# Four edits in a two-block transformer kernel: an own place for the first pair of expert rows, stream banks for memory's values, DVE for the table of rates, heads' steps ahead of channels' steps

## The reference, cut to what matters

```
# first block: mixer, then the expert layer
h   = rmsnorm(x, g_mix);   m = rmsnorm(mem, g_mem)
q, k, v, xl, gl, qm, gate = split(h @ w_in);   km, vm = split(m @ w_mem_kv)
y0 = windowed attention(rope(q), rope(k), v, sink)          # 6 heads
xc = depthwise_conv(xl)                                     # 4 taps
log_a = -8 * sigmoid(xc @ w_r + b_r) * softplus(-lam)       # lam: 2 x 768 learned numbers
y1 = gelu(gl) * (scan forward + scan backward of a = exp(log_a), sqrt(1-a^2) * i * xc)
y2 = softmax(qm @ km.T / sqrt(128)) @ vm                    # 4 heads, 256 memory rows
x  = x + (sum of sigmoid(gate_n + b) * (y_n @ p_n)) @ w_out
h2 = rmsnorm(x, g_ffn)                                      # PEER: 8 heads, top 16 of 128 x 128 experts
x  = x + sum over the picked experts e of gate_e * gelu(h2 . u_e) * v_e
# second block, twice: hybrid_layer
x  = rmsnorm(x, g_final)
z  = rmsnorm(x, norm1) @ w_in
ya = retention(4 heads);  yb = 31-tap conv, layer norm, silu;  yc = gelu, layer norm, 256 x 256 mixing;  yd = windowed attention, 8 heads
x  = x + (sum of sigmoid(gate_n) * (y_n @ w_branch_n)) @ w_out
x  = x + (silu(h @ w_gt) * (h @ w_up)) @ w_ffn_out
```

## Time and profile before

| | |
|---|---|
| median of three runs | 2144.68 us (2143.9 to 2147.41) |
| the profiled execution's own time | 2145.49 us |
| its span | 2144.2 us |
| PE busy | 2113.1 us (99%) |
| DVE, ACT, POOL busy | 65%, 58%, 46% |
| mean granted PE clock | 0.998 |

### The profile page before, as it was taken

One profiled execution on the slowest core, in us unless ns is written; L12 is line 12 of the kernel. 1 busy time (PEld: TensorE's weight loads), 2 busy tenths in 40 slices (PEclk: granted clock), 3 DMA queues, 4 the chain that ended last, 5 costly groups with the idle time before them and its releaser, 6 DMA issues.

```text
span 2144.2 us, 37243 instructions
## 1 busy us (share of the span) xinstructions
PE 2113.1 (99%) x14292; PEld 1958.1 (91%) x14292; DVE 1395.7 (65%) x2706; ACT 1247.4 (58%) x2272; POOL 977.1 (46%) x791
## 2 busy tenths in 40 slices
PE   7999999999999999999999999999999999999999
PEld 7999989999999998888889899998888999998887
DVE  4467655998676756666667765557764864757874
ACT  5669454546777865455445465746555465756553
POOL 4776557999667650000004785660001876661000
PEclk9999999999999999999999999999999999999999
DMA  6444565655444456666665554555565645455565
GB/s 231 149 138 129 172 197 173 196 178 180 145 140 147 141 168 204 195 192 192 195 195 196 186 157 139 155 180 167 187 205 158 189 146 168 141 165 177 187 194 160
DMA packets 103952, 370.59 MB, mean 173 GB/s; under 512 B 11480, under 2 KB 12896, under 8 KB 103264
## 3 DMA queue, kind: packets, MB, share of 16 engines
q1 hardware_dynamic: 103776, 368.21, 54.8%
HBM read 366.05 MB, written 2.11 MB: 172 GB/s over the span
## 4 chain that ended last, share of the span: by engine, by line
PE 88%; DVE 6%; ACT 2%; POOL 1%; issue 1%; DMA 1%; SPq 0%; DVEq 0%; ACTq 0%; POOLq 0%
PE stream_bank L568 14%; PE stream_bank L570 14%; PE stream_bank L569 14%; PE side_bank L568 9%; PE side_bank L570 9%; PE side_bank L569 9%; PE side_bank L577 4%; PE stream_bank L577 4%; PE side_bank L574 2%; PE stream_bank L574 2%; PE side_bank L918 1%; PE side_bank L917 1%; POOL unit_lo L2606 1%; ACT unit_hi L1181 1%; PE side_bank L746 1%
## 5 line engine op out<-in xcount | busy, mean ns | idle before, releaser
L2606 POOL TENSOR_TENSOR unit_lo<-raw,unit_hi 128x512 fp32r<-128x512 f32 (+1 forms) x724 | 938.5, 1324 | 943.6 <-ACT unit_hi L1181 941.6
L1181 ACT ACTIVATE unit_hi<-raw 128x1024 fp32r<-128x1024 f32 (+1 forms) x678 | 708.9, 1046 | 199.5 <-PE side_bank L570 66.0
L1777 DVE TENSOR_TENSOR unit_lo<-raw,unit_hi 128x1024 fp32r<-128x1024 f32 (+1 forms) x316 | 390.3, 1236 | 227.9 <-ACT unit_hi L1181 225.9
L568 PE MATMUL stream_bank<-hT,unit_hi 128*128 128x256 f32 x1360 | 398.9, 293 | 1.8 <-POOL unit_lo L2606 1.8
L570 PE MATMUL stream_bank<-hT,unit_lo 128*128 128x256 f32 x1360 | 384.6, 283 | 0.0
L569 PE MATMUL stream_bank<-hT,unit_hi 128*128 128x256 f32 x1360 | 384.5, 283 | 0.0
L568 PE MATMUL stream_bank<-h2T,unit_hi 128*128 128x256 f32 x1024 | 293.3, 286 | 0.0
L570 PE MATMUL stream_bank<-h2T,unit_lo 128*128 128x256 f32 x1024 | 289.8, 283 | 0.0
L569 PE MATMUL stream_bank<-h2T,unit_hi 128*128 128x256 f32 x1024 | 289.6, 283 | 0.0
L568 PEld LDWEIGHTS stream_bank<-hT,unit_hi 128*128 128x128 f32 x1360 | 259.9, 191 | 3.6 <-POOL unit_lo L2606 2.0
L569 PEld LDWEIGHTS stream_bank<-hT,unit_hi 128*128 128x128 f32 x1360 | 260.0, 191 | 1.6
(11 more groups left out here) (392 smaller groups left out, 4303.9 us busy)
## 6 DMA issues: line engine op xcount, KB each, us to landing
raw<-in_peer_u_dram SPq DMA_DIRECT2D x128, 512.0 KB, 3.5
raw<-in_peer_v_dram SPq DMA_DIRECT2D x128, 512.0 KB, 4.1
raw<-in_gate_dram SPq DMA_DIRECT2D x64, 512.0 KB, 3.5
raw<-in_gt_dram SPq DMA_DIRECT2D x44, 512.0 KB, 3.5
raw<-in_up_dram SPq DMA_DIRECT2D x44, 512.0 KB, 3.5
raw<-in_ffn_out_dram SPq DMA_DIRECT2D x44, 512.0 KB, 3.5
raw<-in_branch_dram SPq DMA_DIRECT2D x32, 512.0 KB, 3.5
raw<-in_w_gate_dram SPq DMA_DIRECT2D x24, 512.0 KB, 3.5
```

The lines of the kernel that those rows point to most:

```text
L568: mm(out, l.hi, r.hi, start=start, stop=False)
L1181: activation(k.unit_hi[n % SPLIT_SLOTS][:, 0:w], k.raw[n % RAW_SLOTS][:, 0:w], ACT.Copy).then_inc(k.sem("unit_hi"), 1)
L1777: V.tensor_tensor(k.unit_lo[s][:, 0:w], k.raw[n % RAW_SLOTS][:, 0:w], k.unit_hi[s][:, 0:w], ALU.subtract).then_inc(unit_lo, 1)
L2606: last = G.tensor_tensor(k.unit_lo[s][:, cols], k.raw[n % RAW_SLOTS][:, cols], k.unit_hi[s][:, cols], ALU.subtract)
```

## The change

1. `first_pair` is a pair over `X`; `expert_pair(0)` gives it and `expert_pair(j)` the three old ones. ACT's `expert_hi(0)` waits for the last spreading of gates in place of the last `peer_u` unit, and PE's wait for the last gated row moves from ahead of `peer_v` 0 to ahead of its second token tile. SP waits for unit 0 of `peer_v` before it fetches `X` back.
2. `vm` takes the next two stream banks.
3. The series of the rates moves from POOL to DVE, in rounds 10 to 14 of its LRU side.
4. In a layer, DVE runs `sides` ahead of `own_channels` in each round. PE, ACT and POOL keep their order.

```diff
@@ -395,6 +395,9 @@
 
+    def expert_pair(self, j):
+        return self.epair[j % 3] if j else self.first_pair
+
     def peer_tiles(self, phase):
@@ -407,6 +410,7 @@
         self.epair = [self.pair(f"expert_pair{i}", [P, TOKENS], at=hot + i * 2048) for i in range(3)]
+        self.first_pair = self.pair("first_expert_pair", [P, TOKENS], at=x)
         self.g_final = self.place("g_final", [P, D], at=hot + 8192)
@@ -625,7 +629,7 @@
 
-    def tm_unit(key, i, lhs, first, chunks, width, banks, start, stop, ready=None):
+    def tm_unit(key, i, lhs, first, chunks, width, banks, start, stop, ready=None, late=None):
 
@@ -635,6 +639,8 @@
             for t, h in ends:
+                if late is not None and (t, h) == (1, 0):
+                    pe.wait_ge(*late)
                 last = mm3(banks[t][h][:, 0:wd], lhs.at(lambda x: x[:, first + c, t * P:(t + 1) * P]),
@@ -714,8 +720,12 @@
 
-    def token_major(key, units, chunks, width, lhs, ready=None):
-        banks = [[take(SIDE + t, (key, t))] for t in range(TILES)]
+    def token_major(key, units, chunks, width, lhs, ready=None, in_stream=False):
+        if in_stream:
+            banks = [[take(rotation[(turn[0] + t) % len(rotation)], (key, t))] for t in range(TILES)]
+            turn[0] += TILES
+        else:
+            banks = [[take(SIDE + t, (key, t))] for t in range(TILES)]
         for u in range(units):
@@ -852,7 +862,7 @@
                 yield
-            yield from token_major("vm", 4, 2, 512, k.memT)
+            yield from token_major("vm", 4, 2, 512, k.memT, in_stream=True)
             while "inputs_read" not in at.stages:
@@ -931,13 +941,13 @@
         banks = [[take(SIDE + 2 * t + h, ("peer_v", t, h)) for h in range(2)] for t in range(TILES)]
-        pe.wait_ge(k.sem("unit_gated"), units_gated(KEYS - 1))
         for j in range(KEYS - CLOSING):
-            ep = k.epair[j % 3]
+            ep = k.expert_pair(j)
             pe.wait_ge(k.sem("expert_lo"), j + 1)
             one = ep.at(lambda x: x[:, :].unsqueeze(1))
-            tm_unit("peer_v", j, one, 0, 1, 1024, banks, j == 0, False)
-        close_banks("peer_v", KEYS, lambda j: k.epair[j % 3], lambda j: (k.sem("expert_lo"), j + 1), banks)
+            late = (k.sem("unit_gated"), units_gated(KEYS - 1)) if j == 0 else None
+            tm_unit("peer_v", j, one, 0, 1, 1024, banks, j == 0, False, late=late)
+        close_banks("peer_v", KEYS, k.expert_pair, lambda j: (k.sem("expert_lo"), j + 1), banks)
 
@@ -1369,8 +1379,9 @@
                 act.wait_ge(unit_mm, at.unit)
-                activation(k.vm[:, t, :], k.bank[SIDE + t][:, 0:512], ACT.Identity,
-                           scale=k.small("nm_r", TILES)[:, t:t + 1]).then_inc(k.free[SIDE + t], 1)
+                b = k.bank_of["vm", t]
+                activation(k.vm[:, t, :], k.bank[b][:, 0:512], ACT.Identity,
+                           scale=k.small("nm_r", TILES)[:, t:t + 1]).then_inc(k.free[b], 1)
             while "inputs_read" not in at.stages:
@@ -1477,13 +1488,14 @@
             if j == 0:
-                act.wait_ge(unit_mm, U["peer_u", KEYS - 1] + 1)
+                act.wait_ge(k.sem("gates_mm"), 2 * GROUPS)
                 act.wait_ge(*k.over["gates", GROUPS - 1])
             if j == 1:
+                act.wait_ge(unit_mm, U["peer_u", KEYS - 1] + 1)
                 act.wait_ge(k.sem("unit_gated"), units_gated(KEYS - 1))
...
                 act.wait_ge(unit_mm, U["peer_v", j - 3] + 1)
-            split_hi(k.epair[j % 3].hi[:, :], k.experts[:, j, :], "expert_hi")
+            split_hi(k.expert_pair(j).hi[:, :], k.experts[:, j, :], "expert_hi")
 
@@ -1919,6 +1931,7 @@
         yb, z = k.small("yb", 12), k.small("z", 12)
+        z2, terms = k.small("z2", 12), 9
         a_, b_, i_, t1 = k.lru_a, k.lru_b, k.lru_i, k.lru_t
@@ -1960,9 +1973,20 @@
             own.then(V.tensor_scalar(z, ya, 2.0, None, ALU.add))
-            V.reciprocal(z, z).then_inc(k.sem("lam_inverse"), 1)
-            for _ in range(4):
-                yield
+            own.then(V.reciprocal(z, z))
+            yield
+            own.then(V.tensor_tensor(z, ya, z, ALU.mult))
+            own.then(V.tensor_tensor(z2, z, z, ALU.mult))
+            own.then(V.tensor_scalar(c8, z2, 1.0 / (2 * terms + 1), 1.0 / (2 * terms - 1), ALU.mult, ALU.add))
+            for i in range(terms - 2, -1, -1):
+                own.then(V.tensor_tensor(c8, c8, z2, ALU.mult))
+                own.then(V.tensor_scalar(c8, c8, 1.0 / (2 * i + 1), None, ALU.add))
+                if i % 3 == 0:
+                    yield
+            own.then(V.tensor_tensor(c8, c8, z, ALU.mult))
+            own.then(V.tensor_scalar(c8, c8, 2.0, None, ALU.mult))
+            own.then(V.tensor_tensor(c8, c8, yb, ALU.add))
+            V.tensor_scalar(c8, c8, -LRU_C / 2, None, ALU.mult).then_inc(k.sem("rates"), 1)
             br = COLS["lru_br"][0]
@@ -2548,7 +2572,7 @@
 
-        at.run(main(), [bias_tables() if l == 0 else iter(()), own_channels(), sides()])
+        at.run(main(), [bias_tables() if l == 0 else iter(()), sides(), own_channels()])
         turned = norm_lo(name("n2"), name("norm2"), k.sumT)
@@ -2641,27 +2665,8 @@
 
-        def tables():
-
-            yield from steps(10)
-            ya, yb, c8 = k.small("ya", 12), k.small("yb", 12), k.small("c8", 12)
-            z, z2, terms = k.small("z", 12), k.small("z2", 12), 9
-            pool.wait_ge(k.sem("lam_inverse"), 1)
-            own.then(G.tensor_tensor(z, ya, z, ALU.mult))
-            own.then(G.tensor_tensor(z2, z, z, ALU.mult))
-            own.then(G.tensor_scalar(c8, z2, 1.0 / (2 * terms + 1), 1.0 / (2 * terms - 1), ALU.mult, ALU.add))
-            for i in range(terms - 2, -1, -1):
-                own.then(G.tensor_tensor(c8, c8, z2, ALU.mult))
-                own.then(G.tensor_scalar(c8, c8, 1.0 / (2 * i + 1), None, ALU.add))
-                if i % 3 == 0:
-                    yield
-            own.then(G.tensor_tensor(c8, c8, z, ALU.mult))
-            own.then(G.tensor_scalar(c8, c8, 2.0, None, ALU.mult))
-            own.then(G.tensor_tensor(c8, c8, yb, ALU.add))
-            G.tensor_scalar(c8, c8, -LRU_C / 2, None, ALU.mult).then_inc(k.sem("rates"), 1)
-
         at.run(units(("km", 4), ("vm", 4), ("va", 2), *MIXER_FM, ("gate", 24), ("p_mem", KD // 2), ("p_attn", KD),
-                     ("p_lru", KD)), [tables(), rope()])
+                     ("p_lru", KD)), [rope()])
         for _ in units(("w_out", 8)):
@@ -2795,6 +2800,7 @@
     sp.wait_ge(k.sem("landed_x_out"), 16 * 2 * TILES)
+    sp.wait_ge(k.sem("unit_mm"), U["peer_v", 0] + 1)
     for i, (t, cols) in enumerate(pieces):
...
```

## The result

The changed kernel takes 2161.44 us (median of four runs, 2160.31 to 2162.9) against 2144.29 us before (four runs, 2139.11 to 2147.41): a ratio of 1.0086, 95% interval 1.0074 to 1.0097. It is slower by 17.1 us. The profiled execution took 2162.9 us, its span is 2161.6.

A forecast was written before the change was run, and what follows sets the result against it. TensorE was taken as the bound, busy 2113.1 of 2144.2 us. Mixer 3.4, switch -3.5 and layers 16.6 sum to 16.5 us, giving 2162.0 for the profiled execution and 2161 us as median; range 2136 to 2168.

The forecast's parts named there:

- Values in stream banks: At memory's first `vm` and `va` matmuls: two PE waits and a clock fall go, gain 1.9 + 1.7 + 1.5 = 5.1 us.
- Rates: Before the first LRU matmul: small DVE instructions, many held by POOL, delay the convolutions; +3.4 us for the mixer.
- 0.3 for the last two, which wait for nothing: On DVE: the last two small operations ahead of the convolutions take 0.3 us together, ending at 76.7.
- Switch: Before `peer_v`, at 789.27 us: PE's wait and the clock's fall go, gain 3.5 us; bounds 0 and 3.8.
- the 0.8 feared for SP's later return of `X`: At the first expert pair: unit 4's load is hidden by 1.4 us; if landing takes 6 us, it costs 0.8.
- Layers: Heads' steps first on DVE delay the second gating matmul: 8.0 + 1.7 - 1.4 = 8.3 us a layer, +16.6 for two.
- the lower of the two chains: Rounds near 1324 to 1343, DVE's two-input operations never held by POOL: second gating matmul 7.0 us later; held, 9.6.
- The three eighths of the difference that I added: At the second gating matmul: 3/8 x 2.6 us added to 7.0 for channel operations held by POOL, making 8.0.
- The turning: At 1226.05 us: PE's 1.44 us wait for DVE, which did convolution first, goes; -1.4 us a layer.
- The rival with the rates hidden: Small DVE operations before the LRU matmul get in without waiting, layers slow: +6.2 us, 2151; chance 0.18.
- that of quicker layers: Rates exposed, but in the layers DVE catches up unseen and PE loses two waits each: -4.5 us, 2140; chance 0.15.

The follow-up runs named there:

- first_two: channels_first with the series of rates back on POOL, so only the first pair's own place and the stream banks stay: 2138.79 us.
- values_alone: The kernel before with memory's values in stream banks and nothing else: 2141.2 us.
- rates_alone: The kernel before with only the series of the rates on DVE, its running value in a PSUM bank: 2140.7 us.
- psum_series: channels_first with the running value of the series on DVE in a PSUM bank: 2134.28 us.
- channels_first: The changed kernel with DVE's old order in the layers, channels' steps ahead of heads' steps; the other three edits stay: 2146.4 us.
- retention_first: psum_series with heads' steps ahead of channels' steps on DVE only until the retention heads are done, the old order behind: 2131.75 us.

## Why the prediction was right, and which terms were off

2161 us was forecast and 2161.44 measured; both large losses stand at the predicted places. Term by term, against the table of differences:

- **Values in stream banks**: 5.1 forecast; -0.15 to -5.49, 5.3 measured. That it holds rests on POOL being free: with POOL's series more than half is given back (first_two, values_alone). The prediction didn't name this tie; its sum was right since the series had left POOL. 1.6 of the 5.3 is the clock's fall near 31 us, which rates_alone doesn't have behind the same wait.
- **Rates**: PE's arrival 6.9 us early, 7.4 measured. The durations were right: six at 1.22, six at 0.17 in POOL's pause, own low half done at 62.7 (63.4 forecast), then ten steps to 75.09. The failed step is the one that put the convolutions at 76.7: "0.3 for the last two, which wait for nothing". Both lasted 1.33, so the convolutions began at 77.59, and PE started at 89.92, 2.6 later than before in place of 1.7. (The steps ahead of them came out 1.3 us early: the low half by 0.7, the ten steps at 1.25 instead of 1.3 by 0.5.) That they wait for nothing didn't save them, nor are such instructions always held: beside a working POOL the same two took 0.53 and 0.17 in psum_series and 0.64 and 0.17 in rates_alone. What decides it no run shows. The clock then took 2.7 (+2.62 to +5.36) behind a pause of 10 us, not the 1.7 seen behind one of 1.9. Mixer: +5.4 against +3.4. The expert layer took 0.6 of it back; channels_first, the same kernel up to there, has 0.6 more instead (+4.67 to +5.30), so this differs between executions and is no effect of an edit.
- **Switch**: 3.5 forecast, 3.24 measured; 0.4 of the wait stayed (0.2 left for it), and the clock stayed at 1.00. Near 802 us PE then loses 0.1 to 0.3 us in every kernel with this edit (+1.56 to +1.74 in the changed one) and nothing in values_alone and rates_alone. This is little beside the 0.8 feared for SP's later return of `X`; whether that return is its cause isn't shown.
- **Layers**: 8.3 a layer forecast, 7.6 and 8.0 measured. The four splits of the first layer end at 1329.75, 1333.70, 1339.85 and 1345.14 (forecast 1330.0; 1333.1, 1339.5 and 1345.0 when not held), the product at 1350.53 (1350.3). This is the lower of the two chains: the products' mean was 693 ns, and one of the four was held (1.52 us, the others 0.42). The three eighths of the difference that I added (1.0) were not needed: second gating matmul +7.0 counted from the turning, 8.0 forecast. The clock took 2.2 to 2.6 instead of 1.7. The turning gave 1.6 in place of 1.4, and 1.95 with the next head's by the queries. The second layer's loss was made up otherwise: the clock had fallen already behind the wait of 2.09 for a low half and took 1.6 there, and PE's last wait was 3.5 instead of 5.0.

The errors, +0.9 and +1.0 in the mixer, and -0.7 and -0.3 in the layers, partly cancel, and the drift of -0.6 helped: at the end the changed trace is 17.4 us behind, where 16.5 was forecast. That the medians came within 0.4 us of the forecast is luck; the mechanism, the two places and the sizes to within 2 us are not. The rival with the rates hidden is what psum_series is, and was excluded here by the operands' place; that of quicker layers is excluded by channels_first, which stands 15 us below the changed kernel.

**A faster version.** retention_first keeps all four edits in a form that pays: 2131.75 us, 11.4 below before and 29.7 below the changed kernel (by medians that were not taken side by side).

## What to carry to other kernels

Before small chained work is moved from GpSimd to VectorE, look where its operands are: beside a busy GpSimd each chained instruction that read two SBUF operands, or scaled within SBUF, took up to one whole GpSimd instruction (1.22 us here), and the same one with its running value in PSUM 0.18. An order of two streams in one queue is to be judged by the stretch: the turned order paid 1.95 us a layer where the heads release PE, and cost 9.5 to 9.9 with the clock where a channel's product releases a unit's split, so switch it at the stage. And two edits that each remove a wait of PE can be worth more together than the sum, if one makes room on the engine that the other then runs into.

## What was not expected

- The clock's price behind a pause of PE was not one number: 1.4 us behind 2.6 us, 2.6 behind 3.5, 2.4 and 1.5 behind two of 4.2, 2.2 behind 5.0, 2.9 behind 8.9 (channels_first), 2.7 behind 10.0. Behind pauses near 2 us it fell in some executions and not in others: near 31 us in the kernel before but not in rates_alone, whose PE waited 1.9 us at the same place. In the changed kernel the same wait of 2.1 us for a low half cost nothing in the first layer and 1.6 in the second.
- A `tensor_scalar` that reads SBUF and writes PSUM took 0.17 us in the middle of POOL's work (52.66 in psum_series), while the same from SBUF to SBUF took 1.22.
